# A second channel tile of the input projection in three rounded products, and the first tap of k's convolution on ScalarE

## Reference: what is computed

```
h = x @ w_in[l]                       # 256 x 1024 times 1024 x 3360, fp32
(a_u, a_v, b_qkv, b_z, b_beta, b_decay, c_q, c_k, c_v, c_r, c_g) = split(h)
out_a = spatial_gating(gelu(a_u), gelu(a_v), ...)
# out_b: a short causal convolution over time with 4 taps per channel, then silu,
qkv = silu(causal_short_conv(b_qkv, conv_w))     # y = w[0]*xp[:, 0:t] + w[1]*xp[:, 1:t+1] + ...
q, k, v = split(qkv, 3)                          # 512 channels each
# ... l2 norm of q and k, a gated delta rule in chunks of 64 tokens
out_c = gla(...)                                 # gates through exp, log, cumulative sums
x = layer_norm(alpha * x + concat(out_a, out_b, out_c) @ w_out[l])
```

## Time and profile before

| | |
|---|---|
| median of 3 runs | 2248.55 us (2247.55 to 2249.07) |
| the profiled execution's own time | 2248.24 us, of which the span is 2246.6 us |
| PE busy | 2180.7 us (97%) |
| DVE, ACT, POOL busy | 985.8, 696.3, 93.6 us |
| mixing, layer 0 and layer 1 | from about 211 to 400 us and from about 797 to 990 us |
| attention and experts | from about 1205 us to the end |

### The profile page before, as it was taken

How to read it: one execution, slowest core, us unless ns; L and a number is a source line. 1 busy time by engine, 2 the same in 40 slices (tenths; PEclk the granted TensorE clock), 3 DMA queues, 4 the chain that set the end, 5 groups by cost and what they waited for, 6 DMA issues and landing times. The chain is left out here.

```text
span 2246.6 us, 29987 instructions
## 1 busy us (share of the span) xinstructions
PE 2180.7 (97%) x12257; PEld 1325.8 (59%) x12258; DVE 985.8 (44%) x1397; ACT 696.3 (31%) x1105; POOL 93.6 (4%) x139
## 2 busy tenths in 40 slices
PE   8999999999999999999999999999999999999998
PEld 6887885788788877768887753333333333333332
DVE  4565684666475468546648742111111111112111
ACT  4443332444343353234426642111111111111111
POOL 5000020000000001100002000000000000000000
PEclk9999999999999999999999999999999999999999
DMA  8763421687397442149655579999999999999998
GB/s 295 248 228 104 152 77 54 228 264 242 96 307 243 162 144 96 43 132 295 233 178 160 204 297 422 429 429 428 428 429 428 429 428 428 429 428 429 429 428 356
DMA packets 192725, 632.38 MB, mean 281 GB/s; under 512 B 31280, under 2 KB 127552, under 8 KB 166256
## 3 DMA queue, kind: packets, MB, share of 16 engines
q1 hardware_dynamic: 192624, 630.93, 72.6%
HBM read 629.82 MB, written 1.07 MB: 281 GB/s over the span
## 5 line engine op out<-in xcount | busy, mean ns | idle before, releaser
L412 PE MATMUL banks<-ffn_room 128*128 128x512 f32 x1920 | 453.7, 392 | 0.0
L412 PEld LDWEIGHTS banks<-ffn_room 128*128 128x128 f32 x1920 | 357.6, 188 | 72.6
L529 DVE TENSOR_TENSOR ffn_room<-memory,ffn_room 128x2048 fp32r<-128x2048 f32 x124 | 280.8, 2291 | 97.3 <-ACT ffn_room L489 97.2
L3118 DVE TENSOR_SCALAR attend_words<-banks 128x512 f32<-128x512 f32 x32 | 22.1, 692 | 564.1 <-PE banks L2854 564.1
L489 ACT CAST ffn_room<-memory 128x2048 fp32r<-128x2048 f32 x124 | 232.2, 1903 | 68.3 <-PE banks L430 64.7
L430 PE MATMUL banks<-ffn_room 128*128 128x512 f32 x1056 | 248.2, 390 | 0.3
L2854 PE MATMUL banks<-memory 128*64 128x512 f32 x1088 | 244.4, 598 | 0.0
L430 PEld LDWEIGHTS banks<-ffn_room 128*128 128x128 f32 x1056 | 197.7, 188 | 42.7 <-DVE ffn_room L568 2.1
L2854 PEld LDWEIGHTS banks<-memory 128*64 128x64 f32 x1088 | 75.7, 137 | 151.8 <-issue 149.7
L2854 PE MATMUL banks<-attend_later,memory 128*64 128x512 f32 x672 | 152.1, 594 | 0.1
L495 ACT ACTIVATE memory<-banks 128x256 f32<-128x256 f32 x88 | 33.8, 385 | 344.3 <-PE banks L412 321.3
(11 more groups left out here) (462 smaller groups left out, 2684.6 us busy)
## 6 DMA issues: line engine op xcount, KB each, us to landing
memory<-in_ffn_w SPq DMA_DIRECT2D x132, 1024.0 KB, 7.2
memory<-in_w_gate_up SPq DMA_DIRECT2D x62, 2048.0 KB, 22.2
attend_later<-in_w_gate_up SPq DMA_DIRECT2D x39, 2048.0 KB, 23.5
memory<-in_w_down SPq DMA_DIRECT2D x25, 2048.0 KB, 24.2
attend_later<-in_w_down SPq DMA_DIRECT2D x19, 2048.0 KB, 23.0
attend_words<-in_w_gate_up SPq DMA_DIRECT2D x17, 2048.0 KB, 22.3
memory<-in_w_in SPq DMA_DIRECT2D x32, 1024.0 KB, 6.6
memory<-in_w_ada SPq DMA_DIRECT2D x32, 768.0 KB, 4.9
```

Of the source, the lines that this page charges most:

```text
L412: m = nc.tensor.matmul(psum[:, GU + tt, :], x_parts[:, xp, k, tt * P:tt * P + P], rows, start=(n == 0), stop=(n == 3 * KD - 1))
L529: tt_op(b, chip.ring[:, chip.slot(base + i), :], a.bitcast(F32), ALU.subtract).then_inc(chip.used, 1)
L3118: ts(room.gate, psum[:, GATE_BANK, :], 7.0, None, ALU.min).then_inc(s["g_ready"], 1)
```

## The change

Tile 3 (k's channels) joins the tiles in parts, the two new leading copies are put on ACT between `evac(1)` and `evac(2)`, and the first tap of k's convolution (four multiplications by a number per partition) goes from DVE to ACT, behind `evac(7)`. The list of DVE's rests grows by two with `IN_PARTS`, ahead of `finish_x`. The room `more` lies over words that are written only later (`bk`, `scaled_q`, `qdT`, `u`, half of `ob`).

```diff
-IN_PARTS = (1, 2)
+IN_PARTS = (1, 2, 3)
@@
+    more = rounded("more", w.at, 4096)
@@
-    lead_rooms = (chip.tmp_rounded, free[:, 2048:4096], late[:, 0:2048], late[:, 2048:4096])
+    lead_rooms = (chip.tmp_rounded, free[:, 2048:4096], late[:, 0:2048], late[:, 2048:4096],
+                  more[:, 0:2048], more[:, 2048:4096])
@@ ACT
+            def first_tap(t):
+
+                act.wait_ge(s["evac"], 2 * (t + CHANNELS) + 2)
+                act.wait_ge(s["zeros"], 1)
+                for c in range(4 * t, 4 * t + 4):
+                    m = func(conv[:, c, :], qkvT[:, c, 0:256], ACT.Identity, scale=parT[:, c:c + 1])
+                m.then_inc(s["tap"], 1)
+
@@
             lead(2, 1)
-            for n in range(1, 4):
-                evac(n)
+            evac(1)
+            lead(3, 0)
+            lead(3, 1)
+            evac(2)
+            evac(3)
@@
             silu(0)
             evac(7)
+            first_tap(1)
             decay(0)
@@ DVE
             take_back(0, 4)
-            convolve(1, range(4))
+            dve.wait_ge(s["tap"], 1)
+            convolve(1, range(1, 4))
```

More of the change, by code:

```diff
@@ L720 @@
        "ub_mm wt_mm ub wt scan_a scan_q u_rows scan_o o_rows scan_s state b_ss b_rms b_out "
-       "early_turned early_T b_turned b_T mixed lead low ") + POST_NORM
+       "early_turned early_T b_turned b_T mixed lead low tap ") + POST_NORM
 def mix_loads(chip, l, w_in, w_out):
@@ L3325 @@
 FFN_STEP = 256
-WIDE_SET, SLIM_SET = 102, 32
+WIDE_SET, SLIM_SET = 103, 32
 START = "chain ident x c turned"
```

## The result

| | before | after |
|---|---|---|
| median | 2249.36 us (2247.55 to 2253.37, 6 runs) | 2258.08 us (2254.22 to 2261.73, 6 runs) |
| profiled execution | 2248.24 us | 2261.73 us, of which the span is 2260.1 us |
| ratio after / before | | 1.0040 [1.0030, 1.0051] |

The change makes the kernel slower, by about 9 us (8.7 between the medians; the interval of the ratio lies clear of 1). The profiled execution of after is the longest of its six, so a sum against its profile comes out at 13.5 us, and the 9 us of the medians are the figure to explain. Lines of after are two higher than before in most of the mixing step (L914 is L916, L928 is L930, L1230 is L1232, L1038 is L1040), more further down.

What follows compares the result with a forecast made beforehand. PE bounds the mixing steps, so its gains and losses count one for one, in two layers. Stall + 8.7, gains - 3.2, clock + 4.4 make + 9.9 us on 2248.24; forecast 2258.2 us, range 2253.0 to 2262.5.

Steps and rivals of the forecast that it cites:

- The stall, + 8.7 us: Ahead of unit(4): new ACT copies wait for loads, delaying evac(2); PE stands still 5.1 us in layer 0, 3.6 in layer 1.
- Rival C: Ahead of unit(4): second load lands early enough, no stall, only the gains remain, 2245.3 us; chance 0.07.
- The gains, - 3.2 us: Mixing steps: rounded products in unit(6) and unit(7) give 1.4 us a layer, the tap 0.2; 1.6 a layer in all.
- The clock, + 4.4 us: Behind the idle time ahead of unit(4): PE's clock falls in both layers, 2.2 us each; ends 0 and 5.8 us.
- rival A's half case: Behind the stall: clock falls in layer 0 only, 2256.2 us; chance 0.22 together with A (no fall, 2254.0 us).
- D: ACT ahead of the decays: Identity needs its own table, one more 1.28 us load, covered by idle time; nothing in the sum.
- the tap: k's convolution: takes 1.13 us off DVE ahead of silu(1), but worth only 0.2 us a layer at back(1).
- B: Ahead of cumulate: clock falls there too, and each first fall costs the longest price, + 14.5 us, 2263.0 us; chance 0.09.

Runs made afterwards that it cites:

- the first four experiments: Four of the follow-up kernels, each timed against runs of the kernel before on the same chip; the text does not list which four.
- the kernel with fills: The kernel after, plus matmuls nobody reads on PE ahead of unit(4), ten in layer 0 and six in layer 1: 2260.53 us, ratio 1.0045.

## Why the prediction was right, and where it wasn't

The time (2258.2 forecast, 2258.08 measured) and the side are right, and so is the path: a wait on ACT for loads that have not landed holds up PE's next bank. That the two times meet within 0.1 us is luck. The forecast was 9.65 us above the median of before as it then was (2248.55); measured are 8.7 us, above a median that six runs put at 2249.36. Two terms behind it were too large, the stall by 0.9 us and the clock by 0.9 to 2.6, and one was missing.

- **The stall, + 8.7 us: right in mechanism and in layer 0, somewhat too large in layer 1.** PE's idle time is 4.66 + 2.67 = 7.3 us, but the forecast counted from start to start. Counted so, from the start of the mixing step (210.45 and 801.70 in after, 211.01 and 797.00 before), `unit(4)` starts 4.9 and 2.9 us later, 7.8 in all, where 5.1 and 3.6 were taken. (The whole step begins 0.56 us earlier in layer 0 of after, so clock times can't be held against each other as they stand.) The difference in layer 1 is the landing: the second copy starts at 822.45, 20.75 us into the step, where the prediction's 818.4 is 21.4 us into it. With the loads of w_out moved the stall is 7.1 us. The loads don't land at the same time in each execution (25.2 us into the step `unit(4)` starts here, 26.6 us in the kernel with fills, released by ACT in both), and the stall moves with them. That it goes through whole was right: from `gate_low` on every step of the table is as long as before, or shorter by its forecast gain.
- **Rival C is out.** The copies without a wait, the wait without copies, and the copies in another place all give what the stall's mechanism says: no gap ahead of `unit(4)` without the wait, and a gap with it.
- **The gains, - 3.2 us: right in size and in their parts.** 0.20 at cumulate (0.2 forecast), 1.16 at `c_turn` (1.2), 0.21 at `back(1)` (0.2); 1.6 us a layer in the comparison without stall.
- **The clock, + 4.4 us: right in kind, and not a constant.** The profile of after has 1.8 us in layer 0 and nothing in layer 1 (rival A's half case); other kernels fell in both layers, after shorter idle times. The 1.6 to 2.9 us for one fall were about right: 1.5 to 2.6 us were seen in `unit(4)`.
- **D (a table for Identity) and the tap: right.** The four activations took 1.71 us (1.5 forecast) with no table load ahead of them, and the load ahead of silu(1) had no wait behind it.
- **The missing term.** The prediction looked at PE's gaps in the middle of the mixing step and took all that follows as a mere shift. PE's wait for "issue" at L1038 was in the trace of before, 1.1 us, and went to 4.1 us; a clock fall followed. It wasn't asked what that gap was and whether it can grow. In the medians it takes 2.3 us of after and 2.1 of before, so it nearly cancels in this comparison, as far as runs of different rounds can tell; in the version with copies and rests later it ate the whole gain. **B** (a further fall, ahead of cumulate) didn't come in the profile of after, where 0.93 and 0.91 us of idle time left the clock alone; but it did in one profile, that of the copies without the wait, behind the same 0.93 us.

The sum in measured terms, for the medians: stall and clock together 7.8 + 1.8 = 9.6 us (after) or 7.1 + 3.5 = 10.6 us (the kernel with the moved loads); gains - 3.2 to - 2.2 (the latter is 2244.62 - 2246.81); instructions 2.3 - 2.1 = 0.2. That is between 6.6 and 8.6 us; the medians are 8.7 us apart. The profile's 13.5 us have in addition the gap in layer 1 with the fall behind it, and a longer fall in the attention. Stretches of before, and of after, about 10 us later:

```profile
1320.00:1330.00 10.00, 9.63 (x61) 7.84 (x60) 6.42 (x26) 6.32 (x16) 0.00 (x0) 0.83 1.01 409
1330.00:1340.00 10.00, 9.70 (x47) 4.43 (x48) 3.34 (x14) 2.12 (x7) 0.00 (x0) 1.00 0.07 25
```

```profile
1330.00:1340.00 10.00, 9.63 (x59) 8.18 (x58) 5.95 (x25) 5.81 (x16) 0.00 (x0) 0.77 0.99 397
1340.00:1350.00 10.00, 9.71 (x35) 5.13 (x37) 3.21 (x14) 2.12 (x7) 0.00 (x0) 0.72 0.06 16
```

The work is the same, the clock is not. Why it falls there, with PE busy for 96% of the stretch, stays open. It doesn't take the rounded products: the kernel with the tap alone is only 0.8 us behind the kernel before when it comes from the first mixing step to the attention (986.2 us against 985.4), but its profile reads 0.81 and 0.51 in the two stretches given here of before, and its execution took 2254.32 us, 6.1 more than before's. The spread between runs goes with the clock too. Of the 27 runs of before beside the first four experiments, the 15 with a mean granted clock of 0.998 or more have a median of 2247.2 us, the other 12 one of 2253.1; of the six runs of after, the fastest has the highest mean (0.998) and the three slowest the lowest (0.994 and 0.995). So a difference of 2 us between medians can come from how many of the runs had such falls. Where those falls lie is not shown, as only one run of each kernel has a profile.

## What to carry to other kernels

A copy that waits for a transfer belongs behind every step on its engine that TensorE needs sooner, and the same question is to be asked again for the engine that takes the next step (here DVE's rests). When a step's arithmetic gets shorter, look for the wait that then ends last: of 1.3 us in unit(6), 0.2 came through. And keep bulk loads out of a stretch of many small matmuls: a wait that the profile calls "issue" there can be the engine's own instructions, late behind the loads.

## What the hardware showed beyond that

- Waiting for "issue" in small products: up to 2.7 us at a time beside 2 MB of loads, and none with the loads elsewhere. In layer 1 of after PE resumes 2.6 us after the q8 packet (906.7); what passes in these 2.6 us is open.
- The clock after idle time is no matter of the gap's length alone. It fell behind gaps of 0.93 (copies without the wait, layer 1), 1.52, 2.16, 2.73, 2.88 and 4.66 us, and not behind 0.93 (after), 1.53 (before), 1.74 (with fills) and 2.67 us (after, layer 1). The page "TensorE: Matmul & The Clock Gate" of the Trainium skill, section "What's actually happening", says that the default state is throttled and activity releases it. The falls behind idle time agree with it in kind; the runs here show that the length of a gap alone doesn't tell whether one comes.
- Identity with a factor per partition on ACT, after silu and ahead of the decays, needs no table load: 1.71 us for four times 128x256 words (267.18 in after, right behind `evac(7)`).
